# Two token streams of the last block in one set of matmuls, and one stream's attention steps between the other's

## The reference, cut to what matters

```python
h = rms_norm(x, norm_g[layer]) * (1.0 + scale) + shift      # scale, shift, gate from c, per sequence
# layer 0
q, k, v, g_a, u, g_s = split(h @ w_in_even)                 # 512, 128, 128, 512, 512, 512 wide
o_a = sink_attention(rope(q), rope(k), v, ...)              # chunks of 64, window of 128 before them
o_s = ssm_branch(u, ...)                                    # scan over the tokens, GLU with w_glu
out = concat(o_a * silu(g_a), o_s * silu(g_s)) @ w_out_even
# layer 1
b, c, hv, g_c = split(h @ w_in_odd)                         # 1024 each
out = (silu(g_c) * b * short_conv(c * hv)) @ w_out_odd      # three taps
# after each layer
x = x + gate * out
```

## Time and profile before

| | |
|---|---|
| time, median of 3 runs (lowest, highest) | 2250.7 us (2249.95, 2254.19) |
| time of the profiled execution | 2246.89 us |
| its span | 2245.1 us |
| mean granted TensorE clock | 0.961 |
| PE busy | 2129.9 us (95%) |
| PEld busy | 1656.7 us (74%) |
| DVE, ACT, POOL busy | 818.0, 503.5, 441.9 us (36, 22, 20%) |
| share of the chain that ended last: PE, DVE, DMA | 88%, 4%, 3% |

### The profile page before, as it was taken

One profiled execution on the slowest core, in us unless ns is written; L12 is line 12 of the kernel. 1 busy time (PEld: TensorE's weight loads), 2 busy tenths in 40 slices (PEclk: granted clock), 3 DMA queues, 4 the chain that ended last, 5 costly groups with the idle time before them and its releaser, 6 DMA issues.

```text
span 2245.1 us, 26976 instructions
## 1 busy us (share of the span) xinstructions
PE 2129.9 (95%) x10930; PEld 1656.7 (74%) x10946; DVE 818.0 (36%) x1563; ACT 503.5 (22%) x1047; POOL 441.9 (20%) x313
## 2 busy tenths in 40 slices
PE   8897899899999999999999999999989989999996
PEld 2265767788888767888888578888877758788885
DVE  7536261423335633112345522114251641422222
ACT  1331442322322521001214311002103421200010
POOL 0124414455505001010123010101041001000001
PEclk9998999999999999999999999999988989999998
DMA  8985826788786435554585146554733213344331
GB/s 282 333 241 206 303 82 224 263 298 289 270 275 228 141 111 197 195 187 160 195 264 186 69 167 214 194 191 159 235 114 117 90 38 132 113 150 150 134 137 54
DMA packets 86271, 414.93 MB, mean 185 GB/s; under 512 B 12404, under 2 KB 13460, under 8 KB 51892
## 3 DMA queue, kind: packets, MB, share of 16 engines
q1 hardware_dynamic: 79360, 396.37, 50.3%
q10 hardware_dynamic: 6788, 16.84, 2.6%
HBM read 323.51 MB, written 86.33 MB: 183 GB/s over the span
## 4 chain that ended last, share of the span: by engine, by line
PE 88%; DVE 4%; DMA 3%; POOL 2%; ACT 1%; issue 1%; SPq 0%; DVEq 0%; ACTq 0%; POOLq 0%
PE bank L701 21%; PE bank L703 21%; PE bank L702 21%; PE bank L956 5%; PE bank L645 3%; PE bank L722 2%; PE bank L721 2%; PE bank L915 2%; PE bank L834 1%; PE bank L916 1%; PE bank L792 1%; PE bank L896 1%; DMA ring<-in_ada 1%; PE bank L822 1%; PE bank L765 1%
## 5 line engine op out<-in xcount | busy, mean ns | idle before, releaser
L701 PE MATMUL bank<-p_hh,pair 128*128 128x512 f32 x1952 | 783.0, 401 | 28.6 <-POOL pair L464 15.1
L703 PE MATMUL bank<-p_hh,pair 128*128 128x512 f32 x1952 | 772.5, 396 | 0.0
L702 PE MATMUL bank<-p_hl,pair 128*128 128x512 f32 x1952 | 772.4, 396 | 0.0
L701 PEld LDWEIGHTS bank<-p_hh,pair 128*128 128x128 f32 x1952 | 372.2, 191 | 127.2 <-POOL pair L464 17.8
L702 PEld LDWEIGHTS bank<-p_hl,pair 128*128 128x128 f32 x1952 | 372.3, 191 | 80.9 <-issue 1.4
L703 PEld LDWEIGHTS bank<-p_hh,pair 128*128 128x128 f32 x1952 | 371.7, 190 | 81.5
L464 POOL TENSOR_TENSOR pair<-ring,pair 128x1024 fp32r<-128x1024 f32 x62 | 152.8, 2467 | 208.9 <-ACT pair L455 208.9
L1292 POOL TENSOR_TENSOR pp_mem<-pp_mem 128x512 f32<-128x512 f32 x48 | 62.0, 1292 | 611.6 <-ACT pp_mem L1056 611.5
L1380 POOL TENSOR_TENSOR p_g<-p_t,pp_mem 128x512 f32<-128x512 f32 x32 | 41.3, 1289 | 574.8 <-DVE p_t L1837 574.8
L1711 DVE SCALAR_TENSOR_TENSOR p_x<-bank,mod,p_x 128x512 f32<-128x512 f32 x64 | 47.3, 749 | 261.2 <-PE bank L703 261.2
L1811 DVE TENSOR_TENSOR pp_mem<-p_sw,bank 128x512 f32<-128x512 f32 x32 | 22.0, 689 | 307.4 <-PE bank L703 307.2
(11 more groups left out here) (306 smaller groups left out, 2392.5 us busy)
## 6 DMA issues: line engine op xcount, KB each, us to landing
pair<-parts_scratch SPq DMA_DIRECT2D x198, 1024.0 KB, 4.8
parts_scratch<-pair SPq DMA_DIRECT2D x66, 1024.0 KB, 7.7
ring<-in_dense SPq DMA_DIRECT2D x62, 512.0 KB, 5.5
pair<-ssm_scratch SPq DMA_DIRECT2D x24, 1024.0 KB, 7.4
ring<-in_ada SPq DMA_DIRECT2D x24, 512.0 KB, 4.7
p_H<-in_ada SPq DMA_DIRECT2D x24, 512.0 KB, 4.9
p_x<-in_x SPq DMA_DIRECT2D x4, 2048.0 KB, 25.3
pair<-glu_scratch SPq DMA_DIRECT2D x8, 1024.0 KB, 4.9
```

The source lines that it names most:

```text
L701: pe.matmul(o, ah, bh, start=first, stop=False)
L702: pe.matmul(o, ah, bl, start=False, stop=False)
L703: return pe.matmul(o, al, bh, start=False, stop=last)
```

## The change

In block 4 `project` no longer has a product for each stream. The activations of both lie in one tensor per part (`hh_wide`, `hl_wide`), the sample's 32 columns ahead of the prompt's 512, and each of the three matmuls of a k is done as two of 272 columns (`WCOLS`) with the same weights: 48 matmuls a chunk, none of 32 or 64 columns, and no `join`. A chunk's result takes two neighbouring banks, columns 240 to 511 of the first and 0 to 271 of the second. One hand-written order for all 8 banks (`last_order`, `plan`) takes the place of the six and two in block 4, so four such chunks fit. With `ready`, each k now waits for slice k of both streams. Where ACT and DVE read the same result, DVE now waits until ACT has read it for both streams (`shared_read`). The sample's scores, turned probabilities and attention product stand behind tiles 0, 1 and 2 of the prompt, and its softmax on ACT and DVE moves with them. One memset and its count of the semaphore go. Blocks 1 to 3 keep their products and their six banks; their activations lie in the new tensors.

```diff
-HALVES = [c for c in SPLIT if c != "v" and c not in ("u0", "u1", "u2", "u3")]
+WIDE = [c for c in SPLIT if c != "v" and c not in ("u0", "u1", "u2", "u3")]
+WCOLS = (DEC + TB) // 2
+WAT = 512 - WCOLS
...
     def take(self, pe, blk, name):
         b, _, held = self.uses[blk, name]
-        if held:
-            for what, k in held[1]:
-                self.wait(pe, held[0], what, k)
-        return self.banks[b]
+        for S, b0, freed in held:
+            for what, k in freed:
+                S.wait(pe, b0, what, k)
+        return self.psum[:, 512 * b - 512:512 * b + 512] if self.wide(blk, name) else self.bank(b)
...
-        bank = self.banks[b]
+        if self.wide(blk, name):
+            at = 512 * (b - 1) + WAT + DEC if self.prompt else 512 * b + WAT
+            return self.psum[:, at:at + self.N]
+        return self.bank(b)
...
+def last_order():
+    each = lambda who, names: [(who, n) for n in names]
+    now = each("p", [f"u{t}" for t in range(4)]) + [("s", "u0"), ("p", "nc2-"), ("p", "nb2-")]
+    now += [("w", "k"), ("p", "v"), ("s", "v"), ("w", "q0"), ("w", "q1")]
+    now += [(S, f"ut{a}") for S in "ps" for a in range(4)]
+    now += [(S, f"x{r}{h}") for h in range(2) for r in "ri" for S in "ps"]
+    now += each("w", ["q2", "q3"] + [f"ga{i}" for i in range(4)])
+    now += [(S, f"y{2 * c + a}") for c in range(4) for S in "ps" for a in range(2)]
+    now += each("p", [f"s0_{j}" for j in range(4)])
+    for t in range(4):
+        now += [("w", f"gs{t}")] + each("p", [f"pt{t}_{a}" for a in range(4)])
+        now += each("p", [f"s{t + 1}_{j}" for j in range(4)] if t < 3 else []) + [("p", f"o{t}")]
+        now += each("s", ([f"s0_{j}" for j in range(4)], [f"pt0_{a}" for a in range(4)], ["o0"], [])[t])
+    now += [(S, f"yt{i}") for S in "ps" for i in range(4)]
+    now += [(S, f"{n}{i}") for i in range(4) for S in "ps" for n in ("gl", "a")]
+    now += each("w", [f"out0_{i}" for i in range(8)])
+    now += [(S, n) for n in ("nc1", "nb1") for S in "ps"]
+    now += each("w", [f"{n}{i}" for i in range(8) for n in ("c", "hv", "g", "b")])
+    now += each("w", [f"out1_{i}" for i in range(8)])
+    now += [(S, n) for n in ("nc2", "nb2") for S in "ps"]
+    return now
...
+    at = 0
+    for who, name in last_order():
+        if who == "w":
+            at += at % 2
+            b = at % 8
+            holders = held[b] + held[b + 1]
+            use(sample, 1, name, b, [])
+            use(prompt, NBLK, name, b + 1, holders)
+            held[b] = [(S, blk, S.freed[blk, name]) for S, blk in ((prompt, NBLK), (sample, 1))]
+            held[b + 1] = held[b][:1]
+            at += 2
+        else:
+            S, b = by[who], at % 8
+            blk = 1 if who == "s" else NBLK - 1 if name.endswith("-") else NBLK
+            use(S, blk, name.strip("-"), b, held[b])
+            held[b] = [(S, blk, S.freed[blk, name.strip("-")])]
+            at += 1
...
-        psum = [ctx.enter_context(nc.psum_tensor(f"bank{i}", [P, 512], F32)) for i in range(8)]
-        prompt = Stream(nc, ctx, "p", TB, P, psum[0:6], 0)
-        sample = Stream(nc, ctx, "s", DEC, DEC, psum[6:8], 1)
+        banks = ctx.enter_context(nc.psum_tensor("banks", [P, 8 * 512], F32))
+        psum = [banks[:, 512 * i:512 * (i + 1)] for i in range(8)]
+        full = [sem(f"bank{i}_full") for i in range(8)]
+        prompt = Stream(nc, ctx, "p", TB, P, banks, full, 0)
+        sample = Stream(nc, ctx, "s", DEC, DEC, banks, full, 1)
+        plan(prompt, sample)
...
+        hh_wide = sb("hh", [P, KT, DEC + TB], F32R)
+        hl_wide = sb("hl", [P, KT, DEC + TB], F32R)
+            at = slice(DEC, DEC + TB) if S.prompt else slice(0, DEC)
+            S.hh, S.hl = hh_wide[:, :, at], hl_wide[:, :, at]
...
-            def sample_product(S, b, name, w, ready):
...
+                S, w, o = prompt, [], []
                 for k in range(KT):
                     if ready:
-                        S.wait(pe, b, ready, k + 1)
-                    hi, lo = [x[:, k, :] for x in w]
-                    if k == 0:
-                        pe.matmul(o[:, 0:2 * S.N], hi, S.h[:, k, :], start=True, stop=False)
-                        pe.matmul(o[:, S.N:2 * S.N], lo, S.hh[:, k, :], start=False, stop=False)
-                    else:
-                        pe.matmul(o[:, S.N:2 * S.N], lo, S.hh[:, k, :], start=False, stop=False)
-                        mm = pe.matmul(o[:, 0:2 * S.N], hi, S.h[:, k, :], start=False, stop=(k == KT - 1))
-                mm.then_inc(S.sem["halves"], 1)
-            def project(blk, names, streams, ready=None, freed=None):
-                w = []
-                for S, b in streams(blk):
-                    if not S.prompt:
-                        for n, name in enumerate(names):
-                            sample_product(S, b, name, w[n], ready)
-                        continue
-                    o = []
-                    for k in range(KT):
-                        if ready:
-                            S.wait(pe, b, ready, k + 1)
-                        for n, name in enumerate(names):
-                            if k == 0:
-                                w.append(split_chunk(blk, name))
-                                o.append(S.take(pe, b, name))
-                            hi, lo = [x[:, k, :] for x in w[n]]
+                        for R, b in streams(blk):
+                            R.wait(pe, b, ready, k + 1)
+                    for n, name in enumerate(names):
+                        if k == 0:
+                            w.append(split_chunk(blk, name))
+                            o.append(S.take(pe, blk, name))
+                        hi, lo = [x[:, k, :] for x in w[n]]
+                        if blk < NBLK:
                             mm = three(o[n][:, 0:S.N], (hi, lo), (S.hh[:, k, :], S.hl[:, k, :]), k == 0, k == KT - 1)
                             if k == KT - 1:
-                                mm.then_inc(S.fills(b, name), 1)
-                        if freed and k < KT - 1:
-                            mm.then_inc(S.sem[freed], 1)
+                                mm.then_inc(S.fills(blk, name), 1)
+                            continue
+                        for step, (x, h) in enumerate(((hi, hh_wide), (hi, hl_wide), (lo, hh_wide))):
+                            for half in range(2):
+                                mm = pe.matmul(o[n][:, WAT + WCOLS * half:WAT + WCOLS * (half + 1)], x,
+                                               h[:, k, WCOLS * half:WCOLS * (half + 1)], start=(k == 0 and step == 0),
+                                               stop=(k == KT - 1 and step == 2))
+                                if k == KT - 1 and step == 2:
+                                    mm.then_inc((prompt if half else sample).fills(NBLK if half else 1, name), 1)
+                    if freed and k < KT - 1:
+                        mm.then_inc(S.sem[freed], 1)
...
                             if t + 1 < S.NT:
                                 scores(S, b, t + 1)
                             attend(S, b, t)
-                for S, b in streams(blk):
-                    if not S.prompt:
-                        S.wait(pe, b, "roped", 5)
-                        S.wait(pe, b, "v_ready", 1)
-                        scores(S, b, 0)
-                        turn_probs(S, b, 0)
-                        attend(S, b, 0)
+                        elif t == 0:
+                            S.wait(pe, b, "roped", 5)
+                            S.wait(pe, b, "v_ready", 1)
+                            scores(S, b, 0)
+                        elif t == 1:
+                            turn_probs(S, b, 0)
+                        elif t == 2:
+                            attend(S, b, 0)
...
-                for S, b in streams(blk):
-                    if not S.prompt:
-                        exps(S, b, 0)
-                        turned(S, b, 0)
+                        elif t == 0:
+                            exps(S, b, 0)
+                        elif t == 1:
+                            turned(S, b, 0)
...
-            def join(S, b, *uses):
-                if S.prompt:
-                    return
-                for use in uses:
-                    S.wait_used(dve, b, use)
-                    o = S.banks[S.uses[b, use][0]]
-                    dve.tensor_reduce(o[:, 2 * S.N:3 * S.N], o[:, 0:2 * S.N].rearrange("p (a n) -> p n a", a=2), AX.X, ALU.add)\
-                        .then_inc(S.fills(b, use), 1)
+            def shared_read(S, b, what, k):
+                if S.prompt and b < NBLK:
+                    S.wait(dve, b, what, k)
+                else:
+                    prompt.wait(dve, NBLK, what, k)
+                    sample.wait(dve, 1, what, k)
             def cos_part(S, b, use, n):
-                join(S, b, use)
...
-                S.wait(dve, b, "swapped", n + 1)
+                shared_read(S, b, "swapped", n + 1)
...
                             normalise(S, b, t)
```

(14 more changed lines are left out.)

69 lines of the change are left out of this document (31 added, 38 removed).

## The result

The changed kernel takes 2185.3 us (median of 4 runs, 2181.9 to 2187.9) beside 2252.4 us for the kernel before (4 runs, 2250.0 to 2256.0): ratio 0.970, 95% interval 0.968 to 0.972. The forecast was 2182.3 us. The profiled execution took 2184.6 us, its span is 2182.8.

What follows compares the result with a forecast made beforehand. The prediction took PE to bound block 4, the only block altered. Its terms summed to -68.4 us, from the profiled 2246.9 to 2178.5; with 3.8 us up to the median it forecast 2182.3 us, range 2155 to 2213.

Steps and rivals of the forecast that it cites:

- The products: Block 4's 61 chunks: 48 matmuls of 272 columns at 128.8 ns, 6.18 us a chunk for 7.29; 67.7 us saved.
- The stall behind q3: From q2 to the first y: four double banks shorten PE's wait for q2, 9.0 us in place of 16.2; 7.2 saved.
- Attention: Sample's own tile goes, its work moves between the prompt's tiles, with small waits at gs1 and gs2; 4.6 us saved.
- Turns of y and GLU: Transposes of y behind a busy tile run at full clock, less the GLU's slow start; 4.5 us saved.
- The wait at (c0, hv0): After the norm, PE must wait for the sample's first slice, made behind the prompt's; 11.3 us lost.
- (out1_0, out1_1): PE waits 6.2 us for the sample's split parts, made behind the prompt's eight; 3.6 us lost.
- The last norm: Residual and square lie open, no longer covered by the sample's product; 0.7 us lost.
- blocks 1 to 3 keep their order: Listed among the effects entered at nothing: the blocks before block 4 cost no more than before.
- Rival (a): Matmul pace in block 4: the 15.5 ns are paid per column, 121.6 ns a matmul, 2161 us; chance 0.18.
- its second form: Matmul pace in block 4: the 15.5 ns are not paid at all, 113.3 ns and 2137 us; within the 0.18.
- (c): Block 4's products: load and stream stop overlapping at 272 columns, 155.6 ns a matmul, 2261 us; chance 0.05.
- (d): Block 4: joint waits and bank waits take back the products' gain, needing 68 us of further waits; chance 0.03.

Runs made afterwards that it cites:

- experiment 3: The 544 columns parted as 384 and 160, 304 and 240, or 512 and 32, against the changed kernel's 272 and 272: 2233.0, 2184.2 and 2640.2 us.
- experiment 4: Sample's attention steps moved behind gs1, gs2 and tile 3's turns, against the changed kernel with makers k by k: 2162.2 us beside 2167.3 us.

## Why the prediction came out

The total was right within 3 us. In its terms, each against the profiled executions:

- **The products**: -67.7 forecast, 61 x (7.29 - 6.00) = -78.7 us measured. Mis-sized: the matmul was taken as 128.8 ns, with the 15.5 ns paid for each matmul, and is 125.0, between the two readings (121.6 per column). By the line through 228.8 at 512 and 125.0 at 272 a column costs 0.4325 ns, which is more than the 0.417 of 2.4 GHz, and some 7 ns come with each matmul. The two other partings of experiment 3 gave what that line and the floor forecast, to 1.5 ns a pair. The error was to read the 15.5 ns as one cause or the other; the line has both. (The sample's small matmuls, which the prediction has at some 109 ns, lie 112 ns apart but for the first, which is 28 ns long.)
- **The stall behind q3**: -7.2 forecast. q2 to the first y is now 45.7 us (1662.19 to 1707.88), 9.7 above six chunks, where it was 16.2 above: -6.5. The wait of 5.7 us ahead of ga2 is the 5.8 of the forecast.
- **Attention**: -4.6 forecast, -2.0 measured (67.2 us from the first scores to the turns of y before, 60.1 after, which is 7.1 less, and 5.2 of these are the four chunks). The waits ahead of gs1 and gs2 were taken as 1.0 us each and are 1.3 and 2.2; the second also takes the clock down, which was not in the sum, 1.4 us. The mechanism was right, as experiment 4 shows by removing it.
- **Turns of y and GLU**: -4.5 forecast, -2.6 measured. The turns took 4.26 us, as forecast; the slow start of the GLU is still there (16 matmuls in 8.83 us, where a later one of its kind has 7.11).
- **The wait at (c0, hv0)**: +11.3 forecast, +12.5 measured: 35.2 us from the norm's sums to the start of the next chunk (1886.46 to 1921.65), 23.2 above two chunks, for 10.7. The idle time was 12.7 us, released by the sample's part, as the forecast had it.
- **(out1_0, out1_1)**: +3.6 forecast, +6.7 measured. From b7's end to the start of the chunk behind the pair the changed kernel takes 21.4 us (2101.81 to 2123.19), 9.4 above two chunks: 7.0 idle and 2.4 at half clock. The kernel before had 2.7 above (17.24 us less 14.58), not the 4.5 of the forecast, which counted 3.3 us of slow matmuls whole where only the excess over full clock is lost; and the wait is 7.0 us for the 6.2 of the forecast, the prompt's parts having taken 6.0 us for the 5.0 of the earlier trace rows.
- **The last norm**: +0.7 forecast, +0.9 measured.

These give -69.7 of the 72.7 us; the rest was not traced. The step that failed in its mechanism is "blocks 1 to 3 keep their order", entered at nothing: the order was kept, but the layout of the tokens was not, and 7 us went there. That the total is right within 3 us is in part luck. The products gained 11.0 us more than forecast, the other six terms together fell short by 9.7 us, 3.0 us of gain have no term, and 10.4 us were lost ahead of block 4: in the profiled executions that makes 6.1 us less gain than forecast (2184.6 for 2178.5). The other 3 us came off because the profiled execution before lies 3.8 us under the median that the forecast was based on, and the one after only 0.7 under its own. Rival (a), 121.6 ns and 2161 us, was half right in its price, and its time was missed by as much again through the waits and the blocks before; its second form, 113.3 ns or a little over, was not seen. (c), the straight line of 155.6 ns, is refuted by 125.0 ns, and (d) by the joint waits, which took back some 20 us and not 68.

## What to carry to other kernels

When two streams are joined in one product, join their makers too: the wait is for the later one at each k, so every loop that fills the operands belongs k outside and streams inside. That alone gave another 17 us on top of the change's, and 5 more came from choosing on which banks' holders a double bank has to wait. Price a change of layout even in the parts whose instructions stay the same: measure the pace of one unchanged matmul before and after. And add up the terms one by one before calling a forecast right: here a total 3 us off held terms that were 11 us off.

## What the runs showed of the hardware

- With the same matmuls in the same order, a matmul of 512 columns took 228.9, 230.0 or 230.4 ns in three layouts of the tensors that it reads. Whether the distance of rows or the tensors' places did it, no run isolates.
- With weights loaded for every matmul, two matmuls of together 544 columns took 250 ns as 272 and 272 or as 304 and 240, 286.7 as 384 and 160, and 346 as 512 and 32.
- A steady stream of 512- and 32-column matmuls kept the clock at the level it found: full for 70 us (1900 to 1970), and then, after a few idle us, 1.2 GHz for 600 us, with PE busy for 493 of 500. It cost 450 us over the changed kernel, where the pace at full clock accounts for 140.
- Beside the scans on VectorE a GpSimd multiplication of 1.3 us took 3.3, and a scan of 2.3 us took 3.3, each of them ending late behind the one that had started before it.
